# Two pieces of weight products at a time on the matmul engine, and then the level work of two slots, in the recurrent layer of a four-layer network

## The chip, the core and the metric

The kernel runs on one core of a Trainium2 chip. Its engines are PE (the matmul engine, TensorE, with its weight loads as a row of their own), DVE (VectorE), ACT (ScalarE), POOL (GpSimd) and SP (SyncE); each takes its own list of instructions in order, and they meet at semaphores. The metric is the time of one execution on the device in microseconds, lower is better. All 64 MB and more of weights are fp32 and come from device memory once.

## The reference

Four layers, each with residual and norms, on 512 rows of 1024: a Mamba-2 mixer, sliding-window attention, a conv/pooling mixer with a feed-forward layer, and an HGRN2 mixer with a feed-forward layer. The change lies in the HGRN2 mixer (the recurrent layer), with 8 heads of 128:

```python
z = h @ w_in
q, f_raw, i, g = jnp.split(z, 4, axis=-1)
f = lb + (1.0 - lb) * jax.nn.sigmoid(f_raw.astype(jnp.float32))
log_f = jnp.log(f)
k = 1.0 - f
...
def step(S, inp):                      # CHUNK = 64 rows at a time
    qt, kt, vt, bt = inp               # bt: running sum of log_f in the chunk
    diff = bt[:, :, :, None, :] - bt[:, :, None, :, :]
    decay = jnp.exp(jnp.where(tril[:, :, None], diff, -jnp.inf))
    scores = jnp.einsum('bhtk,bhsk,bhtsk->bhts', qt, kt, decay)
    o = (jnp.einsum('bhts,bhsv->bhtv', scores, vt)
         + jnp.einsum('bhtk,bhkv->bhtv', qt * jnp.exp(bt), S))
    ...
o = o * lax.rsqrt(jnp.mean(o * o, axis=-1, keepdims=True) + EPS)
o = o * gn_g
o = o.reshape(B, T, D_HG) * jax.nn.silu(g)
return o @ w_out
```

## The kernel before

Activations lie transposed, 128 features by 512 rows in a tile. Every product with a weight is made of three fp32r matmuls of 128x512 on split operands: high x high, high x low, low x high (L631, L632, L633, or L600 to L602 in a layer's first unit). A unit is 256 columns of a weight, two tiles; SP loads it in halves, GpSimd splits it, four halves are in flight.

`granules` is a generator that issues these products; between two of its yields lies a **piece**: half a tile, 12 matmuls, in the recurrent layer's input product. In the layer's output product the first 8 pieces hold 6 matmuls each and the next 8 hold 3. `run(gran, n)` issues n pieces. The four banks gp[0..3] take tiles in turn; DVE frees a bank when it takes the tile out (`bank_read`).

The scores with their decay cannot be factored over a whole chunk. The kernel works in chunks of 128 and takes the scores in 8 parts, called **levels**: level 0 is the diagonal, level s pairs blocks of width 64, 32, ..., 1 with their left neighbours (a level is 8 small fp32 matmuls, 4 for s = 1; L938, L931, L944). Per level DVE forms differences (`level_diff`, L2082, L2083), ACT takes their Exp (L1372), DVE multiplies keys and queries in (`level_products`, L2093, L2094), PE makes the level's products in mp[0] or mp[1] in turn, and DVE copies them under a mask into the scores (`collect`, L2115). On DVE slot m = 8n+s (head n, level s) holds: differences of m+2, products of m+1, then the collect of m.

The layer's loop runs over p = 0 to 4 and, in each, 16 slots. In p = 0 to 3 there is a piece of the input product in every slot, for heads 2p and 2p+1; in p = 4 it is a piece of the output product. From p = 1 on a slot also has the level of heads 2(p-1) and 2(p-1)+1, and beside it, by s:
- s = 1: `output` of the head before (L985, L987, into mp[3]), whose square ACT then takes (L1404)
- s = 2: `turn_k`, three transposes into mp[2] (L953), which ACT copies out (`copy_kt`, L1391, semaphore kt_ready) and goes on to `query_exp` (L1385, L1386)
- s = 3: `head_sum` of the head before (L994), also into mp[2]; ACT then takes Ln and Exp of it (`head_root`, L1077, L1079, with a table load ahead of each), and DVE the head's value from that (L2150, L2154). Its high part is ACT's (L1056), its low part DVE's (L1497), and the output product needs both
- s = 5: `states` (L963), into mp[2] again, from which DVE takes the states (`recur`, L2139 to L2144)
- slots 14 and 15 of p < 4: `turn_v` of the two heads that were just projected (L973), in mp[2], each copied out by ACT (`copy_vt`, L1398, semaphore vt_ready). On ACT a table load also stands ahead of Ln for the forget gate (L1365) and ahead of the Exp of the level behind it.

The order on every engine is the order in which the code issues; there is no scheduler.

Of the kernel before, what the change touches and what calls it, by code (L numbers as in the profile page):

```python
# [58 lines left out]
HH = 8  # L59
# [133 lines left out]
def build(nc, x, positions, pre_norm, post_norm, ssm_w_in, ssm_conv_w, ssm_conv_b, ssm_dt_bias,  # L193
# [50 lines left out]
    with ExitStack() as ctx:  # L244
# [324 lines left out]
        def _(pe):  # L569
# [69 lines left out]
            def h_granules(name, norm, lead=0, after_first=None):  # L639
                return granules(name, lambda k: hh[:, k, :], lambda k: hl[:, k, :], lambda k: split0[norm] + k,  # L640
                                lead, after_first)

            def run(gran, n=None):

                if n is None:
                    for _ in gran:
                        pass
                else:
                    for _ in range(n):
                        next(gran, None)  # L650

            def sum_squares(r):

                pe.wait_ge(sq_added, (KT - 1) * (r + 1))
                pe.matmul(mp[3][:, :], ones[:, :], sqsum[:, :], start=True, stop=True).then_inc(sum_ready, 1)
# [257 lines left out]
            def hgrn():  # L913
                gran = h_granules("hg", "pre4", LEAD["hg"], lambda: sum_squares(pre_round[4]))

                def level(n, s):

                    m = 8 * n + s
                    b, j = n // 2 % 2, n % 2
                    if m >= 2:  # L920
                        pe.wait_ge(lv_read, m - 1)
                    if s:
                        pe.wait_ge(x_ready, 7 * n + s)
                    else:
                        pe.wait_ge(hb_ready, n + 1)
                        tile_taken(pe, tiles_of("hg")[0] + 8 * (n // 2) + j)
                    x = XL[:, (7 * n + s - 1) % 3, :]
                    w = LEVELS[s - 1] if s else 0
                    for c in range(NCH):
                        if s == 1:  # L930
                            mm = pe.matmul(mp[m % 2][0:HP, c * HP:(c + 1) * HP], x[:, c * P:c * P + HP],  # L931
                                           x[:, c * P + HP:(c + 1) * P], start=True, stop=True)
                            continue
                        for half in range(2):
                            rows = slice(half * HP, (half + 1) * HP)
                            at = c * P + half * HP
                            if s == 0:
                                mm = pe.matmul(mp[m % 2][rows, at:at + HP], hk[:, b, j, at:at + HP],  # L938
                                               hq[:, b, j, at:at + HP], start=True, stop=True)
                            else:  # L940
                                left = x[:, at:at + HP]
                                right = left.rearrange("p (n k w) -> p n k w", k=2, w=w)[:, :, 1, :]
                                to = c * HP + half * (HP // 2)
                                mm = pe.matmul(mp[m % 2][rows, to:to + HP // 2], left, right, start=True, stop=True)  # L944
                    mm.then_inc(lv_ready, 1)

                def turn_k(n):
                    pe.wait_ge(ke_ready, n + 1)
                    pe.wait_ge(vt_ready, 2 * (n // 2 + 1))
                    if n:  # L950
                        pe.wait_ge(hs_ready, n)
                    for c in range(NCH - 1):
                        mm = pe.transpose(mp[2][:, c * P:(c + 1) * P], Ke[:, c, :], ident)  # L953
                    mm.then_inc(kt_turned, 1)

                def states(n):
                    b, j = n // 2 % 2, n % 2
                    pe.wait_ge(kt_ready, n + 1)
                    if n:
                        pe.wait_ge(hrstd_ready, n)  # L960
                    for c in range(NCH - 1):
                        cs = slice(c * P, (c + 1) * P)
                        mm = pe.matmul(mp[2][:, cs], Kt[:, c, :], hvt[:, b, j, cs], start=True, stop=True)  # L963
                    mm.then_inc(hst_ready, 1)

                def turn_v(p, j):
                    tile_taken(pe, tiles_of("hg")[0] + 8 * p + 4 + j)
                    if j:
                        pe.wait_ge(vt_ready, 2 * p + 1)
                    elif p:  # L970
                        pe.wait_ge(hs_ready, 2 * p)
                    for c in range(NCH):
                        mm = pe.transpose(mp[2][:, c * P:(c + 1) * P], hvt[:, p % 2, j, c * P:(c + 1) * P], ident)  # L973
                    mm.then_inc(vt_turned, 1)

                def output(n):
                    b, j = n // 2 % 2, n % 2
                    pe.wait_ge(lv_read, 8 * n + 8)
                    pe.wait_ge(hs_ready, n + 1)
                    pe.wait_ge(qe_ready, n + 1)  # L980
                    if n:
                        pe.wait_ge(hscaled, n)
                    for c in range(NCH):
                        cs = slice(c * P, (c + 1) * P)
                        mm = pe.matmul(mp[3][:, cs], hvt[:, b, j, cs], SM[:, n % 2, cs], start=True, stop=(c == 0))  # L985
                        if c:
                            mm = pe.matmul(mp[3][:, cs], St[:, c - 1, :], Qe[:, c - 1, :], start=False, stop=True)  # L987
                    mm.then_inc(ho_ready, 1)

                def head_sum(n):  # L990
                    pe.wait_ge(hsq_ready, n + 1)
                    if n + 1 < HH:
                        pe.wait_ge(kt_ready, n + 2)
                    pe.matmul(mp[2][:, :], ones[:, :], sq[:, n % 2, :], start=True, stop=True).then_inc(hsum_ready, 1)  # L994

                gran_out = granules("hg_out", lambda k: hoh[:, k, :], lambda k: hol[:, k, :],
                                    lambda k: split0["hg"] + k)
                for p in range(HH // 2 + 1):
                    for k in range(16):
                        n, s = 2 * (p - 1) + k // 8, k % 8  # L1000
                        run(gran if p < HH // 2 else gran_out, 1)
                        if p:
                            level(n, s)
                            if s == 1 and n:
                                output(n - 1)
                            elif s == 2:
                                turn_k(n)
                            elif s == 3 and n:
                                head_sum(n - 1)
                            elif s == 5:  # L1010
                                states(n)
                        if p < HH // 2 and k >= 14:
                            turn_v(p, k - 14)
# [15 lines left out]
            conv_pool()  # L1029
            ffn(0, 3)  # L1030
            hgrn()
            ffn(1, 5, turn_out)

# [1197 lines left out]
```

## Time and profile before

| | us |
|---|---|
| median of 3 runs | 1989.01 |
| lowest, highest | 1988.88, 1992.72 |
| the profiled execution, whole | 1990.71 |
| its span | 1988.7 |
| the recurrent layer in it, p = 0 to 3 | about 1302 to 1527 |
| p = 4, and the last head's end | about 1527 to 1582 |
| mean granted clock of PE | 0.977 of full speed |

The span is what the profiler saw from the first to the last instruction; the whole execution has 2.0 us around it. PE is busy in 95% of the span, DVE in 54%, POOL in 46%, ACT in 31%. A row of a matmul shows its start and its length until its result is written, and these overlap: how fast they follow each other is read from the starts.

### The profile page before, as it was taken

To read this page: it belongs to the slowest core of one execution; us is meant where nothing else is said; L and a number is where in the kernel's file an instruction comes from. 1 tells how busy PE (TensorE), PEld (TensorE's weight loads), DVE (VectorE), ACT (ScalarE), POOL (GpSimd) and SP (SyncE) were. 2 spreads that over 40 slices of the span, in tenths; PEclk is the share of its full clock that TensorE was granted. 3 is DMA by queue.
4 is the path that set the end of the run, shared out by engine and by line. 5 is a ranking of instruction groups with operands and counts; after the bars stand their busy time and mean duration, and the time that the engine had idled before them with its cause. 6 is when DMAs were issued, how large, how long until landed. Compare 5 with 4: busy or idle time off the path is not lost.

```text
span 1988.7 us, 24972 instructions
## 1 busy us (share of the span) xinstructions
PE 1880.8 (95%) x9602; PEld 1486.1 (75%) x9602; DVE 1079.9 (54%) x1703; ACT 606.8 (31%) x1080; POOL 905.8 (46%) x912
## 2 busy tenths in 40 slices
PE   7899999897899887899999999999999799999997
PEld 5788877685677665557888888887777588888886
DVE  5888888834777756345333322247777653333202
ACT  4444445513333325032111100035667421111001
POOL 4444443344533146315555555553343255555552
PEclk9999999998999998999999999999999899999998
DMA  8766767485555364947888888896654388888884
GB/s 213 163 145 153 158 146 156 102 176 131 117 112 112 80 132 113 216 90 173 185 198 191 194 191 192 187 205 145 136 128 96 75 186 195 191 196 191 185 187 108
DMA packets 211591, 310.77 MB, mean 156 GB/s; under 512 B 22513, under 2 KB 164753, under 8 KB 211473
## 3 DMA queue, kind: packets, MB, share of 16 engines
q0 software_dynamic: 42912, 149.44, 44.3%
q1 hardware_dynamic: 164000, 153.79, 24.8%
q10 hardware_dynamic: 4560, 5.94, 1.1%
q8 instruction: 77, 1.26, 0.3%
q14 instruction: 42, 0.34, 0.1%
HBM read 153.18 MB, written 2.10 MB: 78 GB/s over the span
## 4 chain that ended last, share of the span: by engine, by line
PE 56%; DVE 2%; ACT 1%; ACTq 1%; issue 1%; POOL 0%; DMA 0%; DVEq 0%; POOLq 0%
PE gp L631 16%; PE gp L632 16%; PE gp L633 16%; PE mp L868 2%; PE mp L944 1%; ACTq L1293 1%; PE gp L600 1%; PE gp L601 1%; PE gp L602 1%; PE mp L985 0%; PE mp L994 0%; POOL sqsum L535 0%; DMA c_s<-c_a 0%; DVE h_sm L2115 0%; ACT L1079 0%
## 5 line engine op out<-in xcount | busy, mean ns | idle before, releaser
L555 POOL TENSOR_SCALAR wh<-stage 128x1024 fp32r<-128x1024 f32 (+2 forms) x298 | 345.8, 1161 | 925.2 <-PE gp L633 886.8
L631 PE MATMUL gp<-hh,wh 128*128 128x512 f32 x1544 | 620.3, 402 | 13.2 <-DVE m_raw L1571 4.9
L632 PE MATMUL gp<-hh,wl 128*128 128x512 f32 x1544 | 603.6, 391 | 0.0
L633 PE MATMUL gp<-hl,wh 128*128 128x512 f32 x1480 | 579.1, 391 | 0.0
L631 PEld LDWEIGHTS gp<-hh,wh 128*128 128x128 f32 x1544 | 291.7, 189 | 82.2 <-issue 18.2
L556 POOL TENSOR_SCALAR wl<-stage 128x1024 fp32r<-128x1024 f32 (+2 forms) x298 | 352.8, 1184 | 0.0
L632 PEld LDWEIGHTS gp<-hh,wl 128*128 128x128 f32 x1544 | 291.9, 189 | 59.3 <-issue 1.2
L633 PEld LDWEIGHTS gp<-hl,wh 128*128 128x128 f32 x1480 | 278.9, 188 | 60.0
L559 POOL DMA_DIRECT2D wl<-stage x298 | 263.8, 885 | 94.7 <-POOL wl L556 84.3
L2010 DVE TENSOR_TENSOR val<-gp,rstd 128x512 f32<-128x512 f32 x44 | 30.4, 691 | 203.9 <-PE gp L633 203.9
L1904 DVE TENSOR_TENSOR xT<-gp,xT 128x512 f32<-128x512 f32 x32 | 22.1, 690 | 212.3 <-PE gp L633 212.3
L631 PE MATMUL gp<-f_h,wh 128*128 128x512 f32 x352 | 137.2, 390 | 0.0
L633 PE MATMUL gp<-f_l,wh 128*128 128x512 f32 x352 | 137.0, 389 | 0.0
L632 PE MATMUL gp<-f_h,wl 128*128 128x512 f32 x352 | 136.9, 389 | 0.0
L1056 ACT ACTIVATE f_h<-val 128x512 fp32r<-128x512 f32 x44 | 27.2, 633 | 277.1 <-DVE val L2016 277.1
L2006 DVE TENSOR_TENSOR sq<-gp,rstd 128x512 f32<-128x512 f32 x44 | 30.2, 691 | 114.2 <-PE gp L633 95.0
L1617 DVE SCALAR_TENSOR_TENSOR m_xs<-m_raw,prm,m_xs 128x512 f32<-128x512 f32 x96 | 86.0, 896 | 2.3
L633 PEld LDWEIGHTS gp<-f_l,wh 128*128 128x128 f32 x352 | 66.1, 188 | 13.8
L631 PEld LDWEIGHTS gp<-f_h,wh 128*128 128x128 f32 x352 | 66.1, 188 | 13.7
L632 PEld LDWEIGHTS gp<-f_h,wl 128*128 128x128 f32 x352 | 66.1, 188 | 13.5
L2016 DVE TENSOR_TENSOR val<-val,sq 128x512 f32<-128x512 f32 x44 | 72.7, 1691 | 0.0
L600 PE MATMUL gp<-hh,wh 128*128 128x512 f32 x128 | 55.6, 434 | 18.0 <-DVE hl L1497 15.6
(322 smaller groups left out, 2775.0 us busy)
## 6 DMA issues: line engine op xcount, KB each, us to landing
wl<-stage POOLq DMA_DIRECT2D x264, 512.0 KB, 5.4
stage<-ffn_w SPq DMA_DIRECT2D x120, 512.0 KB, 4.4
stage<-ssm_w_in SPq DMA_DIRECT2D x32, 512.0 KB, 4.6
stage<-hg_w_in SPq DMA_DIRECT2D x32, 512.0 KB, 4.5
stage<-ssm_w_in SPq DMA_DIRECT2D x32, 256.0 KB, 4.0
stage<-ssm_w_out SPq DMA_DIRECT2D x16, 512.0 KB, 4.8
stage<-att_w_in SPq DMA_DIRECT2D x16, 512.0 KB, 4.4
stage<-cp_w_in SPq DMA_DIRECT2D x12, 512.0 KB, 5.4
```

What stands on the lines that cost most here:

```text
L555: pool.tensor_scalar(wh[:, s, part], stage[:, s, part], 1.0, 1.0, ALU.mult, ALU.mult).then_inc(hi_done, 1)
L556: pool.tensor_scalar(wl[:, s, part], stage[:, s, part], -1.0, 1.0, ALU.mult, ALU.mult).then_inc(neg_done, 1)
L559: pool.dma_start(wl[:, s, part], stage[:, s, part], accum_op=ALU.add).then_inc(lo_landed[s], 16)
L600: pe.matmul(bank[:, :], wvh[:, cols], hi(k), start=(k == 0), stop=False)
L631: pe.matmul(bank[:, :], wvh[:, cols], hi(kk), start=start, stop=False)
L632: pe.matmul(bank[:, :], wvl[:, cols], hi(kk), start=False, stop=False)
L633: mm = pe.matmul(bank[:, :], wvh[:, cols], lo(kk), start=False, stop=stop)
L868: mm = pe.matmul(mp[t % 2][b * CB:(b + 1) * CB, :], taps[:, m, t, b, :], shifted[t % 3][:, b, m * SHIFTS:m * SHIFTS + L], start=(m == 0), ...
L1617: ins = dve.scalar_tensor_tensor(v, raw[:, n % 2, i:i + L], prm[:, col:col + 1], v, ALU.mult, ALU.add)
L2006: dve.tensor_tensor(sq[:, j, :], gp[t % 4][:, :], rstd[:, :], ALU.mult).then_inc(bank_read[t % 4], 1)
L2010: dve.tensor_tensor(value_slot(n0 + 2 * n + j), gp[t % 4][:, :], rstd[:, :], ALU.mult).then_inc(bank_read[t % 4], 1)
L2016: dve.tensor_tensor(value, value, sq[:, j, :], ALU.mult).then_inc(value_ready, 1)
```

## The change

The loop over the slots issues two pieces in the even slots and none in the odd ones. The level of an even slot, with what stands beside it, and that of the odd slot behind it then follow each other without a piece between them. The number of pieces per p is the same, 16. DVE, ACT, POOL and SP keep their lists.

```diff
--- before.py
+++ after.py
@@ -998,7 +998,8 @@
                 for p in range(HH // 2 + 1):
                     for k in range(16):
                         n, s = 2 * (p - 1) + k // 8, k % 8
-                        run(gran if p < HH // 2 else gran_out, 1)
+                        if k % 2 == 0:
+                            run(gran if p < HH // 2 else gran_out, 2)
                         if p:
                             level(n, s)
                             if s == 1 and n:
```

On PE in p = 1, head 1, slots 2 and 3: L944 is a level, L953 turn_k, L994 the head sum; L631, L632, L633 are a piece. Before:

```order
L944 MATMUL mp<-h_x 64x32 [waits x_ready,lv_read]
...
L953 MATMUL mp<-cst,h_ke 128x128 [waits hs_ready,vt_ready,ke_ready]
L953 MATMUL mp<-cst,h_ke 128x128 x2
L631 MATMUL gp<-hh,wh 128x512
L632 MATMUL gp<-hh,wl 128x512
L633 MATMUL gp<-hl,wh 128x512
...
L944 MATMUL mp<-h_x 64x32 [waits x_ready,lv_read]
L944 MATMUL mp<-h_x 64x32 x7
L994 MATMUL mp<-sq,ones 128x512 [waits kt_ready,hsq_ready]
```

The same place in the changed kernel:

```order
L633 MATMUL gp<-hl,wh 128x512
L944 MATMUL mp<-h_x 64x32 [waits x_ready,lv_read]
L944 MATMUL mp<-h_x 64x32 x7
L953 MATMUL mp<-cst,h_ke 128x128 [waits hs_ready,vt_ready,ke_ready]
L953 MATMUL mp<-cst,h_ke 128x128 x2
L944 MATMUL mp<-h_x 64x32 [waits x_ready,lv_read]
L944 MATMUL mp<-h_x 64x32 x7
L994 MATMUL mp<-sq,ones 128x512 [waits kt_ready,hsq_ready]
```

The piece of 12 matmuls that stood between turn_k and the next level is now ahead of the first level, so that between turn_k and the head sum only a level is left.

On PE at the end of p = 0, the two turns of v (L973). Before:

```order
L973 MATMUL mp<-cst,h_vt 128x128 [waits bank_read1]
L973 MATMUL mp<-cst,h_vt 128x128 x3
L631 MATMUL gp<-hh,wh 128x512
...
L973 MATMUL mp<-cst,h_vt 128x128 [waits vt_ready,bank_read2]
```

In the changed kernel:

```order
L633 MATMUL gp<-hl,wh 128x512
L973 MATMUL mp<-cst,h_vt 128x128 [waits bank_read1]
L973 MATMUL mp<-cst,h_vt 128x128 x3
L973 MATMUL mp<-cst,h_vt 128x128 [waits vt_ready,bank_read2]
L973 MATMUL mp<-cst,h_vt 128x128 x3
```

Here the last piece of p = 0 moved ahead of the first turn. In p = 1 to 3 a level stands between the two turns.

## Rows read from the trace of the kernel before

**Rows 1.** The page: PE busy in the span; the chain's shares by engine.

```profile
PE 1880.8 (95%) x9602; PEld 1486.1 (75%) x9602; DVE 1079.9 (54%) x1703; ACT 606.8 (31%) x1080; POOL 905.8 (46%) x912
...
PE 56%; DVE 2%; ACT 1%; ACTq 1%; issue 1%; POOL 0%; DMA 0%; DVEq 0%; POOLq 0%
```

**Rows 2.** Stretches (columns in the first line): p=2 with heads 2 and 3; p=4.

```profile
core 0: us, PE busy (x) PEld busy (x) DVE busy (x) ACT busy (x) POOL busy (x), PEclk, DMA share, GB/s
1436.00:1468.00 32.00, 32.00 (x249) 25.02 (x248) 25.69 (x54) 22.13 (x31) 13.44 (x12) 1.00 0.62 133
1528.00:1582.00 54.00, 42.47 (x378) 30.87 (x376) 38.84 (x91) 27.89 (x42) 11.89 (x13) 0.90 0.39 93
```

**Rows 3.** PE's waits in the recurrent layer: total us, times, longest us.

```profile
PE gp L631 <- DVE h_ol L1497: 4.4, 1, 4.4
PE mp L944 <- DVE h_x L2094: 3.6, 2, 3.3
```

**Rows 4.** PE in order of time (start us, us, [idle before <-releaser]): borders of a level.

```profile
1449.72 0.39 PE L633 MATMUL gp<-hl,wh 128*128 128x512 f32 x1
1450.04 0.66 PE L944 MATMUL mp<-h_x 128*64 128x32 f32 x16
1450.62 0.50 PE L631 MATMUL gp<-hh,wh 128*128 128x512 f32 x1
1450.96 0.39 PE L632 MATMUL gp<-hh,wl 128*128 128x512 f32 x1
1451.19 0.40 PE L633 MATMUL gp<-hl,wh 128*128 128x512 f32 x1
```

**Rows 5.** PE, p=3: turn_k and turn_v, each with the matmul behind it.

```profile
1442.40 0.55 PE L953 MATMUL mp<-cst,h_ke 128*128 128x128 f32 x3
1442.71 0.48 PE L631 MATMUL gp<-hh,wh 128*128 128x512 f32 x1
...
1458.36 0.66 PE L973 MATMUL mp<-cst,h_vt 128*128 128x128 f32 x4
1458.77 0.47 PE L631 MATMUL gp<-hh,wh 128*128 128x512 f32 x1
```

**Rows 6.** PE, p=4: turn_k, output, head sum, a late level, the last head's.

```profile
1535.01 0.55 PE L953 MATMUL mp<-cst,h_ke 128*128 128x128 f32 x3
...
1552.21 0.71 PE L985 MATMUL mp<-h_sm,h_vt 128*128 128x128 f32 x4
...
1557.02 1.13 PE L994 MATMUL mp<-sq,ones 128*128 128x512 f32 x2
...
1566.67 0.66 PE L944 MATMUL mp<-h_x 128*64 128x32 f32 x16 [3.26 <-DVE h_x L2094]
...
1570.62 1.22 PE L985 MATMUL mp<-h_sm,h_vt 128*128 128x128 f32 x4 [0.91 <-DVE h_sm L2115]
...
1574.65 2.07 PE L994 MATMUL mp<-sq,ones 128*128 128x512 f32 x2 [0.69 <-ACT sq L1404]
```

**Rows 7.** ACT: a copy of turn_v, then p=4's copies, Exp and Ln.

```profile
1459.05 0.60 ACT L1398 ACTIVATE h_vt<-mp 128x512 f32<-128x512 f32 x1 [1.26 <-PE mp L973]
...
1535.60 0.49 ACT L1391 ACTIVATE h_kt<-mp 128x384 f32<-128x384 f32 x1 [1.32 <-PE mp L953]
...
1538.62 0.69 ACT L1077 ACTIVATE root<-mp,eps_col 128x512 f32<-128x512 f32 x1 [0.20 <-PE mp L994]
...
1555.95 0.47 ACT L1391 ACTIVATE h_kt<-mp 128x384 f32<-128x384 f32 x1
...
1557.08 0.63 ACT L1372 ACTIVATE h_x<-h_x 128x512 f32<-128x512 f32 x1 [0.15 <-DVE h_x L2083]
1557.73 1.28 ACT L1077 ACT_TABLE_LOAD   x1
1559.03 0.69 ACT L1077 ACTIVATE root<-mp,eps_col 128x512 f32<-128x512 f32 x1
```

**Rows 8.** DVE: reading out L6 to products for the next L1; p=4's L5 products.

```profile
1426.78 0.75 DVE L2115 COPY_PREDICATED h_sm<-h_mask,mp 128x256 f32<-128x256 uint32 x1
...
1427.92 1.15 DVE L2059 TENSOR_SCALAR h_k<-h_b 128x512 f32<-128x512 f32 x1
1428.99 0.41 DVE L2082 TENSOR_TENSOR h_x<-h_b 128x256 f32<-128x256 f32 x1
...
1430.32 0.74 DVE L2115 COPY_PREDICATED h_sm<-h_mask,mp 128x256 f32<-128x256 uint32 x1 [0.58 <-PE mp L944]
...
1431.50 0.86 DVE L2082 TENSOR_TENSOR h_x<-h_b 128x256 f32<-128x256 f32 x1
...
1432.95 0.41 DVE L2094 TENSOR_TENSOR h_x<-h_x,h_q 128x256 f32<-128x256 f32 x1
...
1566.11 0.41 DVE L2094 TENSOR_TENSOR h_x<-h_x,h_q 128x256 f32<-128x256 f32 x1
```

## The prediction

> **What bounds the kernel now.** I read the page first, then the table of stretches, then the waits of PE inside the recurrent layer, then the rows of PE, ACT and DVE at the places that the change touches. PE is busy for 95% of the span, and more than half of the chain that ended last is PE's [rows 1]. So a microsecond saved on PE is a microsecond of the kernel wherever PE waits for nobody, and nothing elsewhere. The recurrent layer has both kinds of place. In p=1 to 3 (the stretch shown is p=2, levels of head 3) PE is busy all of the time (32.00 of 32.00 us), with DVE at 25.69 us and ACT at 22.13 us; in p=4, where a piece has 6 or 3 matmuls in place of 12, PE is busy for 42.47 of 54.00 us [rows 2], and its waits in the layer lie there, 3.6 us for level operands of DVE and 4.4 us for the last head's low part among them [rows 3]. So p=0 to 3 is set by PE's own row of work, and p=4 by the chain over ACT and DVE.
>
> **The change, part by part.** Nothing is added or removed: the same matmuls, DVE, ACT, GpSimd and DMA work. On PE a piece moves ahead of the level of the even slot before it. I call a slot's level L0 to L7.
>
> 1. A change of kind goes. Inside a piece matmuls start every 0.23 us. From its last matmul to a level it is 0.32 us (1449.72 to 1450.04), and the first matmul after a level takes 0.34 us to the next (1450.62 to 1450.96) [rows 4]. A piece that no longer stands between two levels saves 0.09 + 0.11 = 0.20 us. There are 24 pairs in p=1 to 3 and one in p=0 (between the two turns of v): 25 x 0.20 = 5.0 us gained. The 8 pairs of p=4 are dealt with below.
>
> 2. The head sum now waits for a copy. turn_k (L953) writes bank mp[2], ACT copies it (copy_kt), and only then may the head sum (L994) write that bank. Before, a piece of 2.7 us lay between; now only L3 does. turn_k's result is there 0.55 us after its start, the copy starts 0.04 us later and takes 0.49 us (1535.60), and PE starts about 0.15 us after a release (1566.11 + 0.41 to 1566.67): 1.23 us [rows 6 to 8]. PE gets there in 0.31 us (turn_k) + 0.59 us (L3) = 0.90 us [rows 4, 5]. The stall is 0.33 us, in five heads of p=1 to 3: 1.6 us lost. Behind the head sum on PE stand the next two pieces, and nobody else waits for them soon.
>
> 3. The second turn of v waits for a copy too, in the same bank. Its first turn lasts 0.66 us, ACT's copy starts 0.03 us later and takes 0.60 us, and 0.15 us more make 1.44 us; PE arrives after 0.41 + 0.59 = 1.00 us [rows 4, 5, 7]. 0.44 us x 3 = 1.3 us lost. In p=0 no level lies between the two turns: 1.44 - 0.41 = 1.03 us lost once. These durations assume that ACT is free when the bank is written. It has had two pieces (5.5 us) for its queue by then; its longest queue, two table loads of 1.28 us with two activations of 0.63 us, is 3.8 us [rows 7]. If the cover fails, a table load (1.28 us) more is the price at a place.
>
> Sum for p=0 to 3: -5.0 + 1.6 + 1.3 + 1.0 = -1.1 us. It can't gain more than 5.0. For the other bound, 24 levels could each wait; that is the slower rival. I take -0.8: the nine stalls are worked out for an ACT that starts at once, and 0.03 us more at each is little to ask.
>
> 4. The second level of a pair needs its operands sooner. L(2i+1) follows L(2i) at once, and DVE's products for it come after DVE has read L(2i-2) and L(2i-1) out. Take the tightest pair, L6 and L7 of an even head and L0 and L1 of the next. From reading L6 (1426.78) to the end of the products for L1 (1433.36) are 6.6 us, less the 0.58 us that DVE only waited for L7: 6.0 us of work, two collisions with GpSimd among it [rows 8]. After the change PE needs from L6's end 0.59 (L7) + 24 x 0.23 + 0.20 + 0.61 (L0) = 6.9 us. The margin is 0.9 us, so I cost this at nothing; the work that hides it is the two pieces, and if it fails the whole excess stalls PE.
>
> 5. In p=4 the chain starts one piece later. It runs: turn_k, copy_kt, two small activations, a level's Exp, a table load, Ln, table load, Exp, the head's value on DVE, then all level work behind it. In the first round (turn_k of head 6, sum of head 5) turn_k ends at 1535.56; Ln starts at 1538.62, after 0.20 us of waiting for the head sum [rows 6, 7]. turn_k now has one more piece of 6 matmuls ahead (1.37 us), one change of kind less (-0.2), and what p=0 to 3 gained (-0.8): +0.4 us; less the 0.20 of slack: +0.2 us. In the second round (turn_k of head 7, sum of head 6) the piece has 3 matmuls (0.69 us), and Ln (1559.03) started with the head sum's result long there (1557.02 + 1.13 = 1558.15), so it is ACT's queue that sets it. The slack in that queue is the 0.15 us that the level's Exp waited (1557.08) and some 0.14 us between turn_k's end and the copy (1555.95), which stands behind another Exp [rows 6, 7]: +0.4 us. After that L6, L7 and the last output wait for DVE either way (3.26 us for L6 now, [rows 6]), and the chain carries its delay to the end. The 8 changes of kind that go in p=4 are not counted, since PE waits there.
>
> Sum: +0.2 + 0.4 = +0.6 us. Against the profiled execution's 1990.71 us (span 1988.7 and 2.0 around it) this gives 1991.3 us. The median of the runs shown is 1.70 us below that execution, so the forecast is 1989.6 us. Downstream, the feed-forward layer starts with the last head either way, and the weights for it are staged by then.
>
> **Where the Trainium skill bears on it.** A change of kind costs 0.20 us by [rows 4]. The Trainium skill, "TensorE: Matmul & The Clock Gate", Step-by-step, says that the next tile's weights are pulled ahead and load under the matmul that runs. If that held here without exception, step 1 would gain nothing and the sum would be +5.6 us; the rows show the 0.20 us, so the trace does not bear it out at these borders.
>
> **Rivals.**
>
> A. Slower, by over 4 us: in p=1 to 3 DVE becomes the pace of the second level. Place: L1, L3, L5 or L7, behind their products. For it: DVE is busy 80% of the time, and an operation that meets GpSimd is long (L2059 at 1.15 us; L2082 at 0.86 against 0.41) [rows 8], and what meets GpSimd will be other operations than now. Against it: the 6.0 us of work in step 4 hold two such meetings already. It decides once DVE's work in such a stretch goes over 6.9 us. A third of the 24 pairs late by one meeting of 0.75 us (1.15 - 0.41) is 8 x 0.75 = 6.0 us, and all of them late by 0.25 us the same. With the +0.6 that is 1995.6 us.
>
> B. Faster, by over 4 us: ACT's copies are early enough, or a border is worth more than 0.20 us, and p=4 absorbs the late start. Then it is -5.0 us + 0.6: 1984.6 us. Against it: steps 2 and 3 come from rows of the very instructions.
>
> C. The clock stays up through the last output. The mean granted clock is 0.90 in the last stretch [rows 2]: after PE's wait of 3.26 us, which its row at 1566.67 shows, it falls from 2.4 to 1.2 GHz. Head 7's sum takes 2.07 us in place of head 6's 1.13, and the output's first matmuls 1.22 in place of 0.71 [rows 6]. Both lie in the chain: 0.9 us, and for the output's seven matmuls of 0.23 us about 1.6 us (an estimate: their time doubled) = 2.5 us. The piece that stands between L6 and L7 moves ahead of L6, so that the long wait shortens by 0.69 us to 2.6 and L7 waits longer instead. If the clock then falls only in the final wait, the result is 1989.6 - 2.5 = 1987.1 us, within 0.2% all the same. The Trainium skill's page on TensorE, "HAM oscillation", says that it is unbroken idling that brings the clock down, and by that rule this rival is the likely one. I give it less, since total idling there is no less than before. The clock may as well fall sooner, for about +2 us.
>
> D. No change at all beyond the noise, -0.5 to +0.5 us: the same bucket as the forecast.
>
> **How the numbers follow.** What a measurement of this kernel can tell from no change is about 0.2%, 4 us, and the three runs shown themselves reach from 1988.88 to 1992.72. Chances: the forecast with D 0.55, C 0.22 (either sign), A 0.15, B 0.08. Forecast, C and D all lie within 0.2%; A is mostly beyond and so is B. That gives faster 0.08, same 0.78, slower 0.14. The range takes in C in full and half of the way to A, and stops before B: 1986.0 to 1994.5. The likeliest case's own range is 1988.5 to 1992.
>
> **What would show it.** Right: in p=1 to 3 PE rows with two levels 0.6 us apart; a wait of PE's L994 for ACT's h_kt of about 0.3 us each and of L973 for h_vt of 0.4 (1.0 once); the start of p=4's first level about 0.6 us later than now (one piece of 1.37 more, less 0.8); the last head's low part, and with it PE's release, about 0.6 us later. Wrong: a wait of L931 or L944 for h_x before p=4 (A), the two copies with no wait (B), level work in p=4 that ends over 2 us earlier or later, or a last head sum of 1.13 us in place of 2.07 (C).

## The result, and the profile after

| | before | changed |
|---|---|---|
| median of 7 runs each | 1989.22 us (1987.29 to 1993.5) | 1996.74 us (1995.77 to 1997.91) |
| profiled execution; its span | 1990.71; 1988.7 us | 1996.74; 1994.8 us |

The ratio of the two kernels' runs is 1.0029, with a 95% interval of 1.0019 to 1.0039: the changed kernel is about 5.8 us slower, clear of the measurement's own width. (The medians stand 7.5 us apart, the profiled executions 6.0 us.) The forecast was 1989.6 us, no change, and its range ended at 1994.5. Lines of kernel.py are one higher in the changed kernel from L1001 on (L2094 is now L2095, L2093 is L2094).

The page of the changed kernel, the rows that answer to [rows 1]:

```profile
PE 1877.4 (94%) x9602; PEld 1492.4 (75%) x9602; DVE 1095.9 (55%) x1703; ACT 606.3 (30%) x1080; POOL 901.1 (45%) x912
...
PE 55%; DVE 3%; ACT 2%; ACTq 1%; issue 1%; DMA 0%; DVEq 0%
```

PE's busy time is 3.4 us less and DVE's 16.0 us more, with the same instructions. The chain has gained DVE. The stretches of [rows 2], with the same columns:

```profile
1436.00:1468.00 32.00, 29.49 (x240) 23.81 (x239) 29.04 (x53) 22.00 (x30) 12.62 (x12) 1.00 0.57 125
1528.00:1582.00 54.00, 43.05 (x424) 34.27 (x422) 41.67 (x94) 26.89 (x41) 14.71 (x17) 0.92 0.38 89
```

In the first stretch PE now stands still for 2.51 us where it was never idle, and DVE is busy for 29.04 us with one instruction less than in its 25.69 us before: its instructions got longer. What PE waits for in the recurrent layer (total us, times, longest), against [rows 3]:

```profile
PE mp L944 <- DVE h_x L2095: 13.7, 6, 2.6
...
PE mp L973 <- ACT h_vt L1399: 1.4, 4, 0.8
```

L944 waited twice for 3.6 us; now it waits six times for 13.7. Three of the six lie in p=1 to 3, each in the same place: L3 of the odd head (heads 1, 3 and 5), 2.32 to 2.33 us. Head 3's, on PE (start us, us, then the idle time before it and its releaser):

```profile
1445.09 0.66 PE L944 MATMUL mp<-h_x 128*64 128x32 f32 x16
1445.68 0.55 PE L953 MATMUL mp<-cst,h_ke 128*128 128x128 f32 x3
1448.54 0.66 PE L944 MATMUL mp<-h_x 128*64 128x32 f32 x16 [2.32 <-DVE h_x L2095]
```

L2 starts at 1445.09 and turn_k follows at 1445.68. In head 2, where nobody waits, the level behind turn_k starts 0.47 us after it:

```profile
1414.92 0.55 PE L953 MATMUL mp<-cst,h_ke 128*128 128x128 f32 x3
1415.39 0.66 PE L944 MATMUL mp<-h_x 128*64 128x32 f32 x16
1416.14 1.10 PE L994 MATMUL mp<-sq,ones 128*128 128x512 f32 x2
```

So L3 of head 3 could start at 1446.15. It starts at 1448.54, 2.39 us late, of which the profile shows 2.32 as idle. DVE at that time (L2083 and L2084 are a level's differences, L2094 and L2095 its products):

```profile
1443.24 0.69 DVE L2083 TENSOR_TENSOR h_x<-h_b 128x256 f32<-128x256 f32 x1
1443.85 1.26 DVE L2084 TENSOR_TENSOR h_x<-h_b 128x256 f32<-128x256 f32 x1
1445.03 0.41 DVE L2094 TENSOR_TENSOR h_x<-h_x,h_k 128x256 f32<-128x256 f32 x1
1445.37 3.03 DVE L2095 TENSOR_TENSOR h_x<-h_x,h_q 128x256 f32<-128x256 f32 x1
```

And GpSimd (POOL), a unit's second operation, its DMA and the next unit:

```profile
1443.63 1.20 POOL L556 TENSOR_SCALAR wl<-stage 128x1024 fp32r<-128x1024 f32 x1
1445.13 0.88 POOL L559 DMA_DIRECT2D wl<-stage  x1 [0.30 <-POOL wl L556]
1445.74 1.37 POOL L555 TENSOR_SCALAR wh<-stage 128x1024 fp32r<-128x1024 f32 x1
1446.75 1.36 POOL L556 TENSOR_SCALAR wl<-stage 128x1024 fp32r<-128x1024 f32 x1
```

One product of 0.41 us takes 3.03 us. It starts at 1445.37 and ends at 1448.40, 0.29 us after GpSimd's second operation ends (1446.75 + 1.36 = 1448.11): it is held over both. In the kernel before the same two engines did this in head 3:

```profile
1445.55 0.41 DVE L2093 TENSOR_TENSOR h_x<-h_x,h_k 128x256 f32<-128x256 f32 x1
1445.88 0.41 DVE L2094 TENSOR_TENSOR h_x<-h_x,h_q 128x256 f32<-128x256 f32 x1
1446.22 1.48 DVE L2132 TENSOR_TENSOR h_qe<-h_qe,h_q 128x384 f32<-128x384 f32 x1
```

```profile
1445.31 0.88 POOL L559 DMA_DIRECT2D wl<-stage  x1 [0.30 <-POOL wl L556]
1445.92 1.37 POOL L555 TENSOR_SCALAR wh<-stage 128x1024 fp32r<-128x1024 f32 x1
1447.17 1.45 POOL L556 TENSOR_SCALAR wl<-stage 128x1024 fp32r<-128x1024 f32 x1
```

GpSimd's pair came at the same time, but the product for L3 was through at 1446.29. What met GpSimd was a query product that no level waits for, it took 1.48 us, and a piece of 2.7 us still lay between L2 and L3 on PE. One thing stays unexplained here: the key product at 1445.55 stands just where the held one stands now, 0.24 us behind the DMA issue and 0.37 us ahead of the pair, and took 0.41 us (the same in heads 1 and 5). So the place alone doesn't decide that an operation is held.

**Where the 6 us are.** I measure from the layer's first sum of squares on PE (1301.70 before, 1301.89 now).

| us from there to | before | now | difference |
|---|---|---|---|
| p=4's first level (L938) | 226.77 | 233.17 | +6.40, of which 1.37 is the piece now ahead of it: +5.03 |
| head 7's sum (L994) | 272.95 | 280.54 | +7.59: p=4 adds +2.56 |
| PE's release by the last low part | 280.74 | 288.32 | +7.58 |

From the release to the end of the span the changed kernel is 1.67 us shorter, so 0.19 + 7.58 - 1.67 = 6.1 us, the difference of the spans. By heads, from one L938 to the next:

| us | 0 | 1 | 2 | 3 | 4 | 5 |
|---|---|---|---|---|---|---|
| before | 29.25 | 32.51 | 31.69 | 32.51 | 31.69 | 31.13 |
| now | 28.17 | 34.32 | 30.70 | 34.36 | 30.71 | 33.26 |

```profile
1513.60 0.66 PE L944 MATMUL mp<-h_x 128*64 128x32 f32 x16 [2.33 <-DVE h_x L2095]
1514.18 1.18 PE L994 MATMUL mp<-sq,ones 128*128 128x512 f32 x2
1514.75 1.05 PE L631 MATMUL gp<-hh,wh 128*128 128x512 f32 x1
1515.59 0.63 PE L632 MATMUL gp<-hh,wl 128*128 128x512 f32 x1
...
1518.80 0.39 PE L631 MATMUL gp<-hh,wh 128*128 128x512 f32 x1
```

Eight matmuls start 0.43 us apart in place of 0.23. From the head sum to the matmul at 1518.80 it is 4.62 us, and the same stretch in head 3 takes 3.04 us: 1.6 us. After the equally long waits of heads 1 and 3 the clock did not fall here (granted 1.00 behind both).

### The profile page after: what moved, and what is told of

The parts are those of the page before. It is cut to its first block, busy times and chain, and to the rows that moved or that the text cites. A ratio compares the mean times of both kernels' runs of the same rounds, so it can differ in the third digit from the quotient of the medians.

```text
span 1994.8 us, 24972 instructions
## 1 busy us (share of the span) xinstructions
PE 1877.4 (94%) x9602; PEld 1492.4 (75%) x9602; DVE 1095.9 (55%) x1703; ACT 606.3 (30%) x1080; POOL 901.1 (45%) x912
## 3 DMA queue, kind: packets, MB, share of 16 engines
q8 instruction: 77, 1.26, 0.3%
## 4 chain that ended last, share of the span: by engine, by line
PE 55%; DVE 3%; ACT 2%; ACTq 1%; issue 1%; DMA 0%; DVEq 0%
PE gp L631 16%; PE gp L632 16%; PE gp L633 16%; PE mp L868 1%; PE mp L944 1%; PE gp L600 1%; PE gp L602 1%; PE gp L601 1%; ACTq L1294 1%; DVE h_x L2095 1%; PE mp L994 0%; PE mp L985 0%; DVE h_sm L2116 0%; PE mp L963 0%; DVE h_x L2084 0%
## 5 line engine op out<-in xcount | busy, mean ns | idle before, releaser
L631 PE MATMUL gp<-hh,wh 128*128 128x512 f32 x1544 | 619.2, 401 | 13.0 <-DVE m_raw L1572 4.9
L632 PE MATMUL gp<-hh,wl 128*128 128x512 f32 x1544 | 605.1, 392 | 0.0
L633 PE MATMUL gp<-hl,wh 128*128 128x512 f32 x1480 | 580.2, 392 | 0.0
L631 PEld LDWEIGHTS gp<-hh,wh 128*128 128x128 f32 x1544 | 292.4, 189 | 81.6 <-issue 16.0
L632 PEld LDWEIGHTS gp<-hh,wl 128*128 128x128 f32 x1544 | 292.8, 190 | 60.4 <-issue 1.2
L633 PEld LDWEIGHTS gp<-hl,wh 128*128 128x128 f32 x1480 | 279.8, 189 | 60.1
L631 PE MATMUL gp<-f_h,wh 128*128 128x512 f32 x352 | 137.2, 390 | 0.0
L633 PE MATMUL gp<-f_l,wh 128*128 128x512 f32 x352 | 137.0, 389 | 0.0
L632 PE MATMUL gp<-f_h,wl 128*128 128x512 f32 x352 | 136.9, 389 | 0.0
L633 PEld LDWEIGHTS gp<-f_l,wh 128*128 128x128 f32 x352 | 66.1, 188 | 13.9
L632 PEld LDWEIGHTS gp<-f_h,wl 128*128 128x128 f32 x352 | 66.1, 188 | 13.6
L631 PEld LDWEIGHTS gp<-f_h,wh 128*128 128x128 f32 x352 | 66.1, 188 | 13.6
```

The source lines that it names most:

```text
L631: pe.matmul(bank[:, :], wvh[:, cols], hi(kk), start=start, stop=False)
L632: pe.matmul(bank[:, :], wvl[:, cols], hi(kk), start=False, stop=False)
L633: mm = pe.matmul(bank[:, :], wvh[:, cols], lo(kk), start=False, stop=stop)
```

## The experiments

Each ran on the same chip as the kernel before, whose median there stands beside it. Times are medians; places in the layer are from the profiled execution.

**1. The pairs in p=0 to 3 only.**

```diff
-                        if k % 2 == 0:
-                            run(gran if p < HH // 2 else gran_out, 2)
+                        if p == HH // 2:
+                            run(gran_out, 1)
+                        elif k % 2 == 0:
+                            run(gran, 2)
```

> Two pieces at a time only in p = 0 to 3; p = 4 keeps one piece per slot. Theory 1 (a product of DVE for L3 of heads 1, 3 and 5 is held up by GpSimd's two operations for 2.6 us, and PE with nothing between L2 and L3 waits 2.33 us each time): the three waits of L944 for h_x stay at about 2.3 us, p = 4's first level starts about 5 us later than before, and the median is 4 to 6 us above the kernel before. Theory 2 (the loss lies in p = 4, whose chain over ACT starts a piece late): at most 2 us above before. Theory 3 (order on PE alone, other waits of both kinds): in between, and the waits move to other levels.

Measured: 1997.56 us against 1990.66, ratio 1.003 (1.0016 to 1.0044). The three waits are there with no pair in p=4 (PE's L944 for DVE, from 1300 to 1527 us: 7.0 us, 3 times, longest 2.3). In its profile the clock was at its lower level after two of the three, in heads 1 and 5. There p=4's first level is 6.65 us late; from it to the release it takes 53.98 us, before 53.97. So the whole loss is made in p=1 to 3.

**2. The pairs in p=4 only.**

```diff
-                        if k % 2 == 0:
-                            run(gran if p < HH // 2 else gran_out, 2)
+                        if p < HH // 2:
+                            run(gran, 1)
+                        elif k % 2 == 0:
+                            run(gran_out, 2)
```

> Two pieces at a time only in p = 4. Theory 1 with the chain's late start as a second term: p = 4's first level starts 1.4 us later than before (one piece of 6 matmuls), and PE is released for the last head's weight products 1 to 2.5 us later; the median is 1 to 2.5 us above before. Theory 2 (the whole loss lies in p = 4): 5 to 7 us above. If the clock explains p = 4's part, the head sum of head 7 takes 1.13 us in one of the kernels and 2.07 in the other.

Measured: 1990.71 us, ratio 1.0002 (0.9993 to 1.0012). In the profile the release is 2.59 us late and what follows is 1.6 us shorter, which leaves 1 us that the ratio can't tell from none. Head 7's L6 starts 1.28 us later than before, L7 2.60. The second 1.3 us look like the same hold-up in a milder form: with the last piece ahead of L6, GpSimd's next unit is released sooner and meets the product for L7 (experiment 9 takes 0.9 us of that wait away). In the changed kernel, on DVE and GpSimd:

```profile
1574.20 1.73 DVE L2094 TENSOR_TENSOR h_x<-h_x,h_k 128x256 f32<-128x256 f32 x1
```

```profile
1573.28 1.37 POOL L555 TENSOR_SCALAR wh<-stage 128x1024 fp32r<-128x1024 f32 x1
1574.29 1.36 POOL L556 TENSOR_SCALAR wl<-stage 128x1024 fp32r<-128x1024 f32 x1
```

In the kernel before:

```profile
1567.73 0.42 DVE L2093 TENSOR_TENSOR h_x<-h_x,h_k 128x256 f32<-128x256 f32 x1
```

```profile
1568.48 1.51 POOL L555 TENSOR_SCALAR wh<-stage 128x1024 fp32r<-128x1024 f32 x1 [1.39 <-PE gp L633]
```

**3. All pairs but the one at the waiting place.** Slots 10 and 11 are L2 and L3 of the odd head.

```diff
-                        if k % 2 == 0:
+                        if p < HH // 2 and k in (10, 11):
+                            run(gran, 1)
+                        elif k % 2 == 0:
                             run(gran if p < HH // 2 else gran_out, 2)
```

> The changed kernel, but in slots 10 and 11 of p = 0 to 3 (L2 and L3 of the odd heads) one piece per slot as before. Theory 1: the three waits of 2.33 us are gone, since a piece of 2.7 us lies between L2 and L3 again; the median falls by 6 to 9 us against the changed kernel (7.0 us of waits, and the low clock behind the third), to between 1.5 us below and 1.5 us above the kernel before. Theory 2 (DVE is short of time with pairs in general, and the wait only shows at L3): the wait comes up at another level, and the median falls by under 3 us.

Measured: 1989.29 us, ratio 0.9994 (0.9982 to 1.0006), 8.3 us under experiment 1. All three waits are gone, and no other level waits before p=4. Heads 0 to 4 take 28.17, 31.94, 30.71, 32.15 and 30.71 us, and head 7's sum lies before the old kernel's. One pair in eight made the whole difference.

**4. The other parity: pieces in twos before the odd slots.**

```diff
-                        if k % 2 == 0:
-                            run(gran if p < HH // 2 else gran_out, 2)
+                        if p == HH // 2:
+                            run(gran_out, 1)
+                        elif k % 2 == 1:
+                            run(gran, 2)
```

> Two pieces at a time in p = 0 to 3, but ahead of the odd slots: L1 and L2 stand together, then L3 and L4, L5 and L6, L7 and the next L0; p = 4 keeps one piece per slot. turn_k and the head sum, and the two turns of v, have two pieces between them again, so that no copy of ACT is waited for. If a change of kind is worth what the rows show (0.20 us) and no DVE operation is caught by GpSimd at a bad place, 24 x 0.20 = 4.8 us are gained and the median is 3.5 to 5 us below before. By theory 1 in its general form (a pair leaves DVE a margin of less than one double hold-up of 2.6 us) there are again waits of L944 or L931 for h_x of 1 to 2.5 us, wherever GpSimd's two operations fall on DVE's products, and the median is between 2 us below and 4 us above before.

Measured: 1995.74 us, ratio 1.0021 (1.0008 to 1.0035). The place of the wait moves: L2 of heads 3 and 5 waits 1.58 us, turn_v 0.65 us three times for DVE. The long hold is back on another instruction, a difference (L2086). DVE, then GpSimd:

```profile
1432.23 3.04 DVE L2086 TENSOR_TENSOR h_x<-h_b 128x256 f32<-128x256 f32 x1
```

```profile
1431.99 0.89 POOL L559 DMA_DIRECT2D wl<-stage  x1 [0.30 <-POOL wl L556]
1432.60 1.37 POOL L555 TENSOR_SCALAR wh<-stage 128x1024 fp32r<-128x1024 f32 x1
1433.62 1.37 POOL L556 TENSOR_SCALAR wl<-stage 128x1024 fp32r<-128x1024 f32 x1
```

The pattern is the same to 0.01 us: the DVE instruction starts 0.24 us behind GpSimd's DMA issue, 0.37 us before the pair of operations, and ends 0.28 us behind them. So it is not this product as such that is slow. From the end of the hold DVE works without a pause to the product for L2 (1442.14), and so hands the delay on. Ahead of L2 in head 1 the longest h_x operation takes 1.72 us, and that L2 does not wait. The even heads, which wait for nobody, gain only 0.4 us each here; that was not taken apart.

**5 and 6. GpSimd's operations made small**, in the changed kernel (5) and in the one before (6). For the recurrent layer's input weights but the first two units, GpSimd handles 16 columns in place of the unit's 1024, so the rest of the split into two parts is left out; PE's matmuls and the DMAs stay.

```diff
-                pool.tensor_scalar(wh[:, s, part], stage[:, s, part], ...
-                pool.tensor_scalar(wl[:, s, part], stage[:, s, part], ...
+                few = slice(0, 16) if phases["hg"][0] + 2 <= u < phases["hg"][1] else part
+                pool.tensor_scalar(wh[:, s, few], stage[:, s, few], ...
+                pool.tensor_scalar(wl[:, s, few], stage[:, s, few], ...
```

> The changed kernel, where GpSimd's two operations on each half of the weights of the recurrent layer (all units but its first two) take 16 columns in place of 1024; the rest of the split is left out, so the weights are not split rightly. The semaphores, the DMAs and PE's, DVE's and ACT's work stay. Theory 1 (the waits of 2.33 us come from DVE's products being held up while GpSimd works): the three waits of L944 for h_x ahead of L3 in heads 1, 3 and 5 are gone, no DVE operation of these lines takes over 1 us, and from the first sum of squares to p = 4's first level it is some 6 us less than the changed kernel's 233.2 us: 227 us or less. Theory 2 (DVE or ACT have too much to do between L2 and L3 in any case): waits of over 1 us stay.

> The kernel before with the same small operations of GpSimd (the rest of the split is left out). PE waited for nobody in p = 0 to 3 before, so theory 1 expects from the first sum of squares to p = 4's first level the same 226.8 us as in the kernel before, within 0.3 us; together with the run of the changed kernel with small operations it shows what the order alone is worth: with one more piece of 1.4 us ahead of that level, theory 1 expects the changed order 2 to 4 us ahead here. If instead the order itself costs time, the changed order stays behind.

Measured, one execution each: 1994.77 and 1991.77 us. In 5 the waits of heads 1 and 3 are gone (heads 0 to 4 take 28.17, 32.03, 30.70, 32.03 and 30.71 us). Head 5's wait stayed, 2.33 us, and this is why: GpSimd works there on a unit of the output weights, which was left at full size. DVE and GpSimd in head 5 of this kernel:

```profile
1508.73 3.03 DVE L2096 TENSOR_TENSOR h_x<-h_x,h_q 128x256 f32<-128x256 f32 x1
```

```profile
1508.50 0.88 POOL L560 DMA_DIRECT2D wl<-stage  x1 [0.30 <-POOL wl L557]
1509.11 1.37 POOL L556 TENSOR_SCALAR wh<-stage 128x1024 fp32r<-128x1024 f32 x1
1510.12 1.36 POOL L557 TENSOR_SCALAR wl<-stage 128x1024 fp32r<-128x1024 f32 x1
```

In 6 nothing moved: p=4's first level at 226.78 and head 7's sum at 272.96 us from the layer's start (226.77 and 272.95 in the kernel before). So the old order hides these meetings with GpSimd. The two times themselves say little, since the kernel before took 1983.69 to 1996.12 us in 23 runs beside them; the places in the layer agree to 0.01 us.

**9. The same as 5, with the output weights' units too.**

```diff
-                few = slice(0, 16) if phases["hg"][0] + 2 <= u < phases["hg"][1] else part
+                few = slice(0, 16) if phases["hg"][0] + 2 <= u < phases["hg_out"][1] else part
```

> As the run of the changed kernel with GpSimd's operations cut to 16 columns, but also in the units of the layer's output product (the rest of the split is left out there too). In the run without this, the waits ahead of L3 were gone in heads 1 and 3 and the third, in head 5, was still 2.33 us, with GpSimd's work there on a unit of the output product. Theory 1: now the third is gone as well, p = 4's first level comes 2.4 to 4.5 us earlier than the 228.5 us of that run, and in p = 4 the wait of head 7's L7 falls from 2.2 us to about 1.0, since GpSimd's operations are what stretches DVE's product there; the layer's last head sum comes at or before the 272.9 us of the kernel before. Rival: the third wait is of another kind (the change to the output product), and stays.

Measured, one execution: 1986.56 us beside 1991.71. The third wait is gone; p=4's first level is 2.21 us earlier than before with 1.37 us more ahead of it, so p=0 to 3 gains 3.6 us, and L7 of head 7 waits 1.31 us in place of 2.21. The products for head 5's L3 take 0.42 us each, the second of them:

```profile
1511.94 0.42 DVE L2096 TENSOR_TENSOR h_x<-h_x,h_q 128x256 f32<-128x256 f32 x1
```

That is the changed order without GpSimd in its way, and it settles the cause of the three waits: they are GpSimd's, not DVE's own amount of work. It rests on places in one profile, not on the time of one execution.

**8. GpSimd's operations cut in two**, all work kept: four operations of 512 columns in place of two of 1024, to see whether DVE gets in between. Only the units of the layer's input weights are cut; those of the output weights stay whole.

```diff
-                pool.tensor_scalar(wh[:, s, part], stage[:, s, part], ...
-                pool.tensor_scalar(wl[:, s, part], stage[:, s, part], ...
+                in_hg = phases["hg"][0] <= u < phases["hg"][1]
+                cuts = [(0, (kb - ka) * un.cols)] if not in_hg else [(c * 512, c * 512 + 512) for c in range((kb - ka) * un.cols // 512)]
+                for a, b in cuts:
+                    ins = pool.tensor_scalar(wh[:, s, a:b], stage[:, s, a:b], 1.0, 1.0, ALU.mult, ALU.mult)
+                ins.then_inc(hi_done, 1)
...
```

> The changed kernel, with each of GpSimd's two operations on a half in the recurrent layer cut in two of 512 columns; the same numbers come out. Theory 1, if the hold-up of a DVE operation is as long as the GpSimd operations it meets: DVE gets in between shorter operations, no DVE operation takes over 2 us, and the three waits of PE fall from 2.33 to under 1.2 us; the median is 3 to 6 us below the changed kernel. If DVE is held until the whole row of GpSimd's operations is through, however they are cut, the waits stay at 2.3 us or grow, and the median is within 1.5 us of the changed kernel or above.

Measured: 1997.73 us, ratio 1.003 (1.0017 to 1.0043), no gain in the median. The profile says more, and neither expectation fits it. The waits for L3 in heads 1 and 3 are gone, that of head 5, where the unit is a whole one of the output weights, is still 2.33 us. Other waits come up: L1 of heads 3 and 5 0.69 and 0.67 us, `states` twice 0.54 us. p=4's first level is 4.02 us late with 1.37 us more ahead of it: p=0 to 3 loses 2.65 us, where the changed kernel loses 5.03. Why the median shows none of that is open.

DVE gets in between in some places and not in others. Where a unit stands by itself it does: a difference that meets the two halves of the low part takes 0.83 us. DVE, then GpSimd, in head 1:

```profile
1381.46 0.83 DVE L2089 TENSOR_TENSOR h_x<-h_b 128x256 f32<-128x256 f32 x1
```

```profile
1381.23 1.53 POOL L561 TENSOR_SCALAR wl<-stage 128x512 fp32r<-128x512 f32 x2
```

Where the next unit starts 0.6 us behind the DMA issue, it got in at two such units (1339.19 and 1353.87, 0.76 to 0.92 us an operation), and at six it did not: four differences took 2.71 to 2.87 us, and two scans that otherwise take 1.2 us were held over all four.

```profile
1383.63 3.81 DVE L2070 TENSOR_TENSOR_SCAN h_b<-cst,h_b 128x512 f32<-128x512 f32 x1
```

```profile
1383.67 1.53 POOL L558 TENSOR_SCALAR wh<-stage 128x512 fp32r<-128x512 f32 x2
1384.85 1.51 POOL L561 TENSOR_SCALAR wl<-stage 128x512 fp32r<-128x512 f32 x2
```

The cut operations take longer together (1.53 us for 1.20), so this unit starts 0.71 us behind the start of the product for L3 in place of 0.37, and that product takes its 0.41 us: heads 1 and 3 lost their wait by a shift in time.

**7. A version for both ends**: pairs only where nothing is late. p=4 stays single, slots 10 and 11 too, and 14 and 15 (the turns of v of step 3).

```diff
-                        if k % 2 == 0:
-                            run(gran if p < HH // 2 else gran_out, 2)
+                        if p == HH // 2:
+                            run(gran_out, 1)
+                        elif k in (10, 11, 14, 15):
+                            run(gran, 1)
+                        elif k % 2 == 0:
+                            run(gran, 2)
```

> Two pieces at a time in p = 0 to 3, but one per slot in slots 10 and 11 (L2 and L3 of the odd heads) and 14 and 15 (the two turns of v); p = 4 as before. Theory 1: no wait of PE before p = 4, each of the 18 pairs of levels left gains 0.2 to 0.25 us, p = 4's first level comes 3.5 to 5 us earlier than before, measured from the first sum of squares, and all of it is kept to the end: the median 2 to 5 us below before. Rival: GpSimd catches another product of DVE, waits of 1 to 2.5 us come up, and the median is within 1 us of before or above.

Measured: **1986.07 us against 1991.06, ratio 0.9974 (0.9962 to 0.9986)**: faster than both kernels. PE's two longest waits in its recurrent layer:

```profile
PE gp L631 <- DVE h_ol L1502: 5.1, 1, 5.1
PE mp L944 <- DVE h_x L2099: 3.3, 1, 3.3
```

Neither lies before p=4. p=4's first level is 4.81 us earlier and head 7's sum 4.80, so p=4 keeps all of it. 18 changes of kind at 0.27 us are 4.9 us; two head sums that wait for a copy (0.17 us each, below) take 0.3 back.

## Why the prediction was wrong

**Step 4 failed,** the one on the operands of a pair's second level. It took L6, L7 and the next L0, L1 for the tightest pair, found a margin of 0.9 us with two meetings in it, and costed the second level of a pair at nothing. Two things in it were wrong. The tightest pair is L2 and L3 of an odd head: only turn_k stands between them on PE, and GpSimd works through two units in a row there, so that DVE meets it three times (0.69 and 1.26 us on differences of 0.41, then 3.03 on a product). And the price of a meeting: rival A took 0.75 us from [rows 8]. The hold-up is 3.03 - 0.41 = 2.62 us, since DVE is held over both of GpSimd's operations. The trace of the kernel before has that price, in p=0, where nobody waits for it:

```profile
1337.19 1.99 DVE L2082 TENSOR_TENSOR h_x<-h_b 128x256 f32<-128x256 f32 x1
```

GpSimd's pair runs from 1336.73 to 1338.90 there, and the difference ends 0.28 us behind it. GpSimd's rows and DVE's order of work could have been set against PE's new order, pair by pair, where the text took the sum of DVE's work at one place. That would have shown the risk at L3, not the certainty: in the kernel before the products beside the pair at 1445.92 were not held. Three times 2.4 us of delay are 7.2 us, and the clock's 1.6 us come on top in the profiled execution. The sign that the prediction named for rival A came: waits of L944 for h_x before p=4.

**Rival A was right** in mechanism, place (L3, behind its products) and sign. That its 1995.6 us was 1.1 us off the result is luck: eight meetings of 0.75 us stood for what are three of 2.33, a low clock and a larger gain on PE. It had a chance of 0.15; with "what meets GpSimd will be other operations than now" in its own text, that was too little.

**Step 1** (-5.0 us, "it can't gain more"): the saving is 0.27 us a change of kind, not 0.20. Head 0 has four merges, and gains 1.08 us, turn_k's later border (below) included. Two levels back to back stand 0.52 us apart, where a level alone was counted at 0.59 us:

```profile
1343.54 0.69 PE L938 MATMUL mp<-h_q,h_k 128*64 128x64 f32 x16
1344.06 0.63 PE L931 MATMUL mp<-h_x 128*64 128x64 f32 x8
```

25 of them are 6.75 us. The border between two levels is not in [rows 4], which have a level only between two pieces.

**Steps 2 and 3** had the right sizes. From turn_k to the head sum it takes 1.22 us in heads 2 and 4 (predicted 1.23), and from one turn of v to the next 1.43 or 1.44 us in p=1 to 3 (predicted 1.44):

```profile
1398.58 0.66 PE L973 MATMUL mp<-cst,h_vt 128*128 128x128 f32 x4
1399.16 0.66 PE L944 MATMUL mp<-h_x 128*64 128x32 f32 x16
1400.01 0.63 PE L973 MATMUL mp<-cst,h_vt 128*128 128x128 f32 x4 [0.19 <-ACT h_vt L1399]
```

The profile calls only 0.19 us of the predicted 0.44 a wait, because the level behind the turn starts 0.58 us after it, where a piece started 0.41 us after it; against PE's 1.00 us of before, 0.43 us are lost all the same. Behind turn_k it is 0.47 us for 0.31. Who looks for the predicted wait of L994 finds none in the profile, and has still lost the time. In p=0 the two turns start at 1336.12 and 1337.50; 1.38 us against the 0.35 us that a turn took there is 1.03, as predicted. ACT was free each time. What step 2 had wrong is the number of places: in the three odd heads L3 is late itself, and the copy is there by then.

Put together for p=0 to 3, with turn_k's border already in the 0.27 us, so that a head sum costs another 0.17 us: -6.75 + 2 x 0.17 (heads 2 and 4) + 3 x 0.43 + 1.03 = -4.1 us by the measured prices, where the prediction had -1.1 and took -0.8. With 7.2 us and 1.6 us on the other side it is +4.7, and +5.03 was measured: 0.3 us of p=0 to 3 I can't assign. In experiment 9, where no L3 waits and all five head sums pay 0.17 us, the same prices make -3.6 us, and -3.6 was measured.

**Step 5** (+0.6 us at the end of p=4). With nothing gained ahead of it (experiment 2) L6 of head 7 comes 1.28 us later; the prediction's own terms without its 0.8 us of gain make 1.4. So the delay that it took from the chain over ACT had the right size. It missed the 1.3 us more at L7, which looks like step 4's mechanism again. **Rival C** did not come in this profile: head 7's sum still takes 2.07 us.

```profile
1576.42 1.07 PE L944 MATMUL mp<-h_x 128*64 128x32 f32 x16 [2.21 <-DVE h_x L2095]
...
1582.43 2.07 PE L994 MATMUL mp<-sq,ones 128*128 128x512 f32 x2 [0.69 <-ACT sq L1405]
```

The one long wait was indeed split into 2.57 us (L6) and 2.21 us, but the matmuls behind both are at the lower clock all the same (1.07 us for a level of 0.66 us; the granted clock is 0.50 from 1573.1 to 1584.5). The prediction read "HAM oscillation" in the Trainium skill's page "TensorE: Matmul & The Clock Gate" as speaking for this rival; in this profile the trace does not bear that reading out. But the clock here is not a matter of the order alone. In experiment 3, with the same order in p=4 and L6 and L7 waiting 2.59 and 2.63 us, head 7's sum takes 1.12 us at a granted clock of 1.00, and PE's release comes 6.93 us behind it in place of 7.78: the 0.9 us that rival C counted for it. In experiment 7, with the old order in p=4, it is the same. Whether the changed order makes either more likely, one profile of each kernel can't tell.

**What follows the layer** was taken as unchanged; it was 1.67 us shorter. About 1.2 us are at the start of the output product, where the changed kernel's matmuls stand 0.43 us apart for eight, until 1593.33, and before for fourteen, until 1588.13: six at 0.20 us. Why the clock came back sooner, and the last 0.5 us, stay open. It isn't the order: in the eleven profiles the part behind the release takes either 404.3 to 404.7 or 406.2 to 406.3 us, and experiment 1 has the longer with the same p=4 as experiment 7, which has the shorter.

## What to carry to other kernels

Bundling the work of the engine that sets the pace saves its changes of kind (0.27 us each here), and it takes away the cover between two dependent steps; so go through the pairs one by one and ask of each producer what it may meet while the cover is gone. A mean of busy time, or a sum of work over the stretch, doesn't answer that: here seven pairs of eight were free and the eighth cost more than all of them gained. A meeting is to be priced, as the worst case, at the other engine's whole row of back-to-back operations, and whether it comes can hang on a few tenths of a us (experiment 8). And a partial version (experiment 7) is worth a run even when the whole one is slower.

## What the runs showed of the hardware

- A DVE operation with two inputs in SBUF that starts 0.37 us before a pair of GpSimd operations was held until both were over: 3.03 or 3.04 us for 0.41, in the changed kernel and in experiments 4 and 5, and 3.81 us for 1.2 over four operations (experiment 8). The Trainium skill, "SBUF — State Buffer", section "SBUF: two separate sides", says that DVE and GpSimd share a pair of ports as an exclusive lock, held for a whole instruction; these rows agree that one engine waits, but show the wait lasting over two and four GpSimd instructions.
- Whether such an operation was held over one or over both went with what GpSimd did just before. In the profiles of both kernels and of all experiments but 8, I took the h_x operations (differences and products) of this layer that started up to 0.5 us ahead of a pair of 128x1024 operations, or beside the first of them, and lasted over 0.6 us. 45 met a pair that started up to 0.82 us behind GpSimd's DMA issue for the unit before, and all 45 ended behind the second operation (1.67 to 3.04 us). 39 met a pair with at least 1.28 us between issue and pair, and all 39 were let go behind the first (0.68 to 1.28 us). With the cut operations of experiment 8 the split is not clean. The reason for it the traces don't show, and neither why the products at 1445.55 and 1445.88 in the kernel before were not held at all.
- GpSimd's DMA issue alone held nothing: in experiment 9 a DVE scan takes its usual 1.22 us beside one of 0.88 us.
- A wait of PE of 2.33 us between full streams let the clock fall from 2.4 to 1.2 GHz in one place of three in the changed kernel's profile and in two of three in experiment 1's, with the same order of work there.
